# Gate and up products of the FFN with high and low activation halves as one 512-column operand

## The reference

```
def swiglu(u, wg, wu, wd):
    return (jax.nn.silu(u @ wg) * (u @ wu)) @ wd        # wg, wu: 1024 x 2816, wd: 2816 x 1024
h = h + 0.5 * swiglu(rmsnorm(h, gain), wg, wu, wd)      # first block; the second also norms the result
```

## Time and profile before

| what | value |
|---|---|
| runs | 2073.89 us median of 3 (2067.85 to 2074.85) |
| profiled execution: span, first to last instruction | 2067.1 us; the profile has no time of its own beside it |
| mean granted clock of TensorE | 0.981 of full |
| TensorE, VectorE, ScalarE busy | 95%, 61%, 45% of the span |
| A tiles | 221 DMAs of 1024 KB, 5.7 us from issue to landing |
| B tiles | 181 DMAs of 512 KB, 3.5 us |
| TensorE's waits for act_hl | 1.7 us in all, once |

### The profile page before, as it was taken

How to read it: one execution, slowest core, us unless ns; L and a number is a source line. 1 busy time by engine, 2 the same in 40 slices (tenths; PEclk the granted TensorE clock), 3 DMA queues, 4 the chain that set the end, 5 groups by cost and what they waited for, 6 DMA issues and landing times.

```text
span 2067.1 us, 33713 instructions
## 1 busy us (share of the span) xinstructions
PE 1972.9 (95%) x13218; PEld 1807.7 (87%) x13218; DVE 1256.9 (61%) x1668; ACT 936.1 (45%) x1283; POOL 107.3 (5%) x137
## 2 busy tenths in 40 slices
PE   8999999989998999999999888999999998989998
PEld 7998899989997778999899886799989998878998
DVE  5655655565445546555655698665566555766555
ACT  5444544354445535443544445444454445445443
POOL 0000000000000000000000046100000000010000
PEclk9999999999999999999999998999999999999999
DMA  6444454434452125545444332264445443424442
GB/s 260 186 183 183 147 195 182 173 143 183 183 194 93 50 82 196 199 183 193 171 185 183 140 142 86 82 245 188 187 151 197 183 185 121 143 100 180 191 188 94
DMA packets 60863, 338.35 MB, mean 164 GB/s; under 512 B 6800, under 2 KB 7056, under 8 KB 32384
## 3 DMA queue, kind: packets, MB, share of 16 engines
q1 hardware_dynamic: 59040, 330.00, 42.4%
q0 software_dynamic: 1760, 7.47, 1.1%
HBM read 336.39 MB, written 1.05 MB: 163 GB/s over the span
## 4 chain that ended last, share of the span: by engine, by line
PE 88%; DVE 6%; ACT 3%; DMA 1%; issue 1%; POOL 0%; SPq 0%; DVEq 0%; ACTq 0%
PE X L1312 56%; PE Y L1312 31%; DMA rawA<-in_wa 1%; DVE arena L1147 1%; DVE loA L881 1%; ACT hiA L485 1%; ACT xh L510 1%; PE X L1338 1%; DVE h L942 1%; DVE xl L910 1%; DVE xs L935 0%; POOL rstd L412 0%; ACT Y L495 0%; ACT arena L627 0%; PE Y L1632 0%
## 5 line engine op out<-in xcount | busy, mean ns | idle before, releaser
L1312 PE MATMUL X<-xh,hiA 128*128 128x256 f32 x2944 | 837.5, 284 | 13.0 <-DVE xl L910 11.9
L1312 PE MATMUL X<-xl,hiA 128*128 128x256 f32 x2944 | 836.5, 284 | 0.0
L1312 PE MATMUL X<-xh,loA 128*128 128x256 f32 x2944 | 836.4, 284 | 0.0
L881 DVE TENSOR_TENSOR loA<-rawA,hiA 128x2048 fp32r<-128x2048 f32 x221 | 509.2, 2304 | 309.5 <-ACT hiA L485 309.5
L1312 PEld LDWEIGHTS X<-xh,hiA 128*128 128x128 f32 x2944 | 568.1, 193 | 23.2 <-issue 9.9
L1312 PEld LDWEIGHTS X<-xl,hiA 128*128 128x128 f32 x2944 | 568.1, 193 | 6.2
L1312 PEld LDWEIGHTS X<-xh,loA 128*128 128x128 f32 x2944 | 568.0, 193 | 0.0
L485 ACT ACTIVATE hiA<-rawA 128x2048 fp32r<-128x2048 f32 (+1 forms) x233 | 424.9, 1824 | 81.1 <-PE Y L1312 51.6
L1312 PE MATMUL Y<-hiB,act_hh 128*128 128x512 f32 x704 | 276.8, 393 | 1.7 <-DVE act_hl L990 1.7
L1312 PE MATMUL Y<-loB,act_hh 128*128 128x512 f32 x704 | 275.9, 392 | 0.0
L1312 PE MATMUL Y<-hiB,act_hl 128*128 128x512 f32 x704 | 274.0, 389 | 0.0
(11 more groups left out here) (208 smaller groups left out, 1720.0 us busy)
## 6 DMA issues: line engine op xcount, KB each, us to landing
rawA<-in_wa SPq DMA_DIRECT2D x221, 1024.0 KB, 5.7
rawB<-in_wb SPq DMA_DIRECT2D x181, 512.0 KB, 3.5
row_gain<-in_rows POOLq DMA_DIRECT2D x8, 512.0 KB, 4.6
arena<-in_gla POOLq DMA_DIRECT2D x1, 1280.0 KB, 8.6
h<-in_x SPq DMA_DIRECT2D x2, 512.0 KB, 4.3
rawA<-in_wa SPq DMA_DIRECT2D x2, 512.0 KB, 6.7
out<-h SPq DMA_DIRECT2D x2, 512.0 KB, 2.6
arena<-in_pool POOLq DMA_DIRECT2D x1, 768.0 KB, 7.9
```

What stands on the lines that cost most here:

```text
L881: nc.vector.tensor_tensor(loA[p][:, :], rawA[p][:, :], hiA[p][:, :].bitcast(f32), ALU.subtract).then_inc(a_lo, 1)
L1312: return say(nc.tensor.matmul(*args, **kw))
```

## The change

`xh` and `xl` become the two halves of one buffer `xc`, so that a k-slice's high and low activations lie side by side as 512 columns. For each k-slice of gate and up, one matmul takes these 512 columns against the high weights into a whole PSUM bank, and a second one takes the 256 high columns against the low weights into the right half of the same bank. The sum of the bank's halves is the product. On eviction ScalarE copies the right halves of both banks (gate and up, 2 x 256) to SBUF, and VectorE adds the left halves to them; scaling by `root` is one operation over both (2 x 256). There is no semaphore for gate alone any more. The other stages keep `by_weights`; renamed semaphores and two call sites are left out of the diff.

```
-        xh = sb("xh", [P, KD, TOKENS], f32r)
-        xl = sb("xl", [P, KD, TOKENS], f32r)
+        xc = sb("xc", [P, KD, 2, TOKENS], f32r)
+        xh, xl = xc[:, :, 0, :], xc[:, :, 1, :]
...
+        act_g = arena[:, 12256:13280].rearrange("p (a b c) -> p a b c", b=2, c=TOKENS)
+        act_lo = arena[:, 13280:14304].rearrange("p (a b c) -> p a b c", b=2, c=TOKENS)
...
@@ scalar engine, step of an FFN
+                    act.wait_ge(up_psum, e + 1 + f)
+                    nc.scalar.activation(act_lo[:, p, :, :], X[:, 2 * p:2 * p + 2, TOKENS:512], ACT.Copy
+                                         ).then_inc(part_copied, 1)
                     if s["late"]:
-                        act.wait_ge(gate_scaled, NF * s["deferred"] + 1 + f)
-                        nc.scalar.activation(act_s[:, p, :], act_s[:, p, :], ACT.Silu).then_inc(silu_done, 1)
+                        act.wait_ge(pair_scaled, NF * s["deferred"] + 1 + f)
                     else:
-                        act.wait_ge(gate_psum, e + 1 + f)
-                        nc.scalar.activation(act_s[:, p, :], X[:, 2 * p, 0:TOKENS], ACT.Silu).then_inc(silu_done, 1)
+                        act.wait_ge(parts_added, e + 1 + f)
+                    nc.scalar.activation(act_s[:, p, :], act_g[:, p, 0, :], ACT.Silu).then_inc(silu_done, 1)
@@ vector engine, step of an FFN
                     split_B(b + f, (b + p) % 2)
-                    up = X[:, 2 * p + 1, 0:TOKENS]
+                    dve.wait_ge(part_copied, e + 1 + f)
+                    nc.vector.tensor_tensor(act_g[:, p, :, :], X[:, 2 * p:2 * p + 2, 0:TOKENS], act_lo[:, p, :, :],
+                                            ALU.add).then_inc(parts_added, 1)
                     if s["late"]:
                         if first:
                             dve.wait_ge(root_done, s["deferred"] + 1)
-                        dve.wait_ge(gate_psum, e + 1 + f)
-                        nc.vector.tensor_tensor(act_s[:, p, :], X[:, 2 * p, 0:TOKENS], root, ALU.mult
-                                                ).then_inc(gate_scaled, 1)
-                        dve.wait_ge(up_psum, e + 1 + f)
-                        nc.vector.tensor_tensor(act_h[:, p, :], up, root, ALU.mult).then_inc(up_scaled, 1)
-                        dve.wait_ge(up_scaled, NF * s["deferred"] + 1 + f)
-                        up = act_h[:, p, :]
+                        dve.wait_ge(parts_added, e + 1 + f)
+                        nc.vector.tensor_tensor(act_g[:, p, :, :], act_g[:, p, :, :],
+                                                root.unsqueeze(1).broadcast_to([P, 2, TOKENS]), ALU.mult
+                                                ).then_inc(pair_scaled, 1)
+                        dve.wait_ge(pair_scaled, NF * s["deferred"] + 1 + f)
                     dve.wait_ge(silu_done, e + 1 + f)
-                    dve.wait_ge(up_psum, e + 1 + f)
-                    nc.vector.tensor_tensor(act_h[:, p, :], act_s[:, p, :], up, ALU.mult
+                    nc.vector.tensor_tensor(act_h[:, p, :], act_s[:, p, :], act_g[:, p, 1, :], ALU.mult
                                             ).then_inc(prod_done, 1)
@@ tensor engine
+            def by_pair(bank, wh, wl, k, first, last):
+
+                mm(bank, wh, xc[:, k, :, :].rearrange("p a b -> p (a b)"), start=first, stop=False)
+                return mm(bank[:, TOKENS:512], wl, xh[:, k, :], start=False, stop=last)
...
-            def first_block(s, out_ap, other_ap, done, other_done):
+            def first_block(s, out_ap, other_ap, done, product=by_weights):
...
-                        ins = by_weights(dst, wh[:, j, k, :], wl[:, j, k, :], k, k == 0, k == KD - 1)
-                    if j or done:
-                        ins.then_inc(other_done if j else done, 1)
+                        ins = product(dst, wh[:, j, k, :], wl[:, j, k, :], k, k == 0, k == KD - 1)
+                ins.then_inc(done, 1)
...
-                        ins = by_weights(X[:, 2 * p + j, 0:TOKENS], wh[:, j, k, :], wl[:, j, k, :], k,
-                                         k == 0, k == KD - 1)
-                    ins.then_inc((gate_psum, up_psum)[j], 1)
+                        ins = by_pair(X[:, 2 * p + j, :], wh[:, j, k, :], wl[:, j, k, :], k,
+                                      k == 0, k == KD - 1)
+                    if j:
+                        ins.then_inc(up_psum, 1)
...
-                first_block(s, X[:, 0, 0:TOKENS], X[:, 1, 0:TOKENS], gate_psum, up_psum)
+                first_block(s, X[:, 0, :], X[:, 1, :], up_psum, by_pair)
```

More of the change, by code:

```diff
@@ L244, in build @@
         y_part, h_done = sem("y_part"), sem("h_done")
-        root_psum, root_done, gate_scaled, up_scaled = (sem(n) for n in ("root_psum", "root_done", "gate_scaled", "up_scaled"))
+        root_psum, root_done = sem("root_psum"), sem("root_done")
+        part_copied, parts_added, pair_scaled = sem("part_copied"), sem("parts_added"), sem("pair_scaled")
         vec_chain = sem("vec_chain")
-        gate_psum, up_psum, silu_done = sem("gate_psum"), sem("up_psum"), sem("silu_done")
+        up_psum, silu_done = sem("up_psum"), sem("silu_done")
         prod_done, prod_hi, prod_lo = sem("prod_done"), sem("prod_hi"), sem("prod_lo")
@@ L1666, in hyb @@
                 transposes(s, 1)
-                first_block(s, X[:, 0, 0:TOKENS], X[:, 0, TOKENS:512], None, sg_psum)
+                first_block(s, X[:, 0, 0:TOKENS], X[:, 0, TOKENS:512], sg_psum)
                 pe.wait_ge(phase_loaded["hyb"], 16)
@@ L1798, in gla @@
                 transposes(s, 1)
-                first_block(s, X[:, 0, 0:TOKENS], X[:, 0, TOKENS:512], None, gqk_psum)
+                first_block(s, X[:, 0, 0:TOKENS], X[:, 0, TOKENS:512], gqk_psum)
                 pe.wait_ge(phase_loaded["gla"], 48)
```

## The result

The changed kernel takes 2085.02 us (median of 7, 2083.01 to 2088.64), the one before 2073.89 (2067.44 to 2077.67): ratio 1.0073, 95% interval 1.0059 to 1.0087. It is 0.7% slower, where 2060.4 and faster was forecast.

The account below looks back on a forecast made before the run. TensorE's time per step was taken to bound the FFNs, with eviction counting at their ends. Six late FFNs -11.3, FFN 0 -1.0, FFN 2 -4.2 make -16.5 us; clock +3 gives 2060.4 us, range 2043 to 2084.

Parts of the forecast that it names:

- chain: Eviction after gate and up: from the start of ScalarE's copy to the start of the low part, 3.49 us.
- ring: Repeating eviction and splitting cycle of ScalarE and VectorE inside an FFN: 8.01 us, within TensorE's step of 8.24.
- first wait: First step of a late FFN: TensorE waits 1.7 us for eviction, its down product 1.19 later than before.
- last wait: Last step of an FFN: TensorE waits 2.1 us for the final low part, in FFN 2 1.5.
- the first term: TensorE's gate/up products in each FFN step: a k-slice takes 0.343 us instead of 0.359, saving 0.26 us a step.
- late FFN: FFN with deferred root, 7 of 8; six counted at -1.89 us each: steps -5.20, start +1.19, end +2.12.
- the 3 us allowed for: Clock term: two falls of TensorE's clock behind new waits, 1.7 us of work each, +3; bounds 0 and +24.
- the period: Sign in mid-FFN: TensorE's step repeats every 8.24 us; above 8.34 the prediction is wrong, the saving too small.
- A: Rival: products cost almost nothing beyond their columns, k-slice 0.355; +16 us, with clock +19, 2093 us, slower; chance 0.12.
- B: Rival: the ring is longer than TensorE's step; at 8.3 us it costs 22 us, 2082 us, slower; chance 0.12.
- C: Rival: most new waits are followed by a half-clock stretch, 20 or 24 us, 2077 to 2081 us; chance 0.10.
- D: Rival: k-slice 0.340 and down products at 0.227, saving 0.34 us a step; -30 us, 2044 us; chance 0.14.

Follow-up runs that it names:

- experiment 7: Changed kernel with the second product of each k-slice also taking all 512 columns, low x low added: 2367.67 us, one execution.
- experiment 2: New eviction alone, with three 256-column products per k-slice written into the bank's halves: 2094.94 us, ratio 1.0149 to the kernel before.
- experiment 3: Changed kernel with the 256-column product added into the bank's left half, not the right: 2088.56 us, ratio 1.0083 to the kernel before.

## Why the prediction was wrong

**What was right.** What bounds the kernel; that eviction is hidden in mid-FFN and not at its ends; and the sizes there: chain 3.49 (measured 3.57 and 3.51), ring 8.01 (8.02), first wait 1.7 (1.53 to 1.59), last wait 2.1 (2.05 and 2.06). Only FFN 0's first down product came 0.7 later than summed (31.53 instead of 30.79): its A tile landed 0.7 later (ScalarE begins to split it at 25.21, before at 24.55). The clock fell during that wait of 5.3 us, which is what FFN 0's body lost.

**The step that failed** is the first term: "I take 0.343, nearer to the hopeful end". A k-slice takes 0.3525, so a step saves 0.113 us and not 0.26. In a late FFN that is -2.2 instead of -5.2 in 20 steps, beside +3.5 at its ends (forecast 3.3): +1.3 instead of -1.9. Over eight FFNs, 162 steps that count, it is 24 us, and 2060.4 + 24 = 2084, next to the 2085.02 measured. That the two meet so closely is partly luck. The sum with 0.113 in it puts the profiled execution 10 us above before's, and it is 16.0 above: the clock cost more than the 3 us allowed for (6.4 at last steps alone), FFN 0's start 0.7, and FFN 5 gave 1.3 back. The medians are only 11.1 apart: I had put before's 6.8 us between span and median on the new kernel too, and there it is 1.9. This made up for the clock.

The value lay between the ends I had named, 0.340 and 0.355, near the bad one. Both reasons for the other choice were false. "The first 256 behind a 512 is exactly the neighbourhood" was true of one product (113), not of what follows. And the 0.23 to 0.24 of 512-column products does not come only behind 48 short ones: one short product is enough. The rows held a warning: the short products pay 6.7 ns each in a run (120 against 113), and the first long ones behind them 27 ns in all (2.747 us for twelve against 2.720 in experiment 7). But no row had an alternating stream. Measured, its mean surcharge is 353 - 340 = 13 ns for two products, 6.7 each again; so a removed product saved just one such surcharge, 360 - 353.

Of the signs named, the period did show it, 8.39 where 8.34 was the limit; the last waits stayed at 2.06, and the mean clock came to 0.975, just at its limit.

By the formula of the Trainium skill (TensorE: Matmul & The Clock Gate, "Back-to-back issue gap"), which the page calls the gap of an isolated matmul, a saved product was estimated at 2.5 ns. Measured are 6.7, so it is too small here, but its direction, that merging is worth little and the sum comes out slower, was the better guide.

**The rivals.** A is nearest to what happened: its mechanism with a slice of 0.355, its size too large (2093). Its turning point, a saving of 0.16 us a step, fits: 0.113 is below it, and the kernel is slower. B didn't occur, with 0.37 us to spare instead of 0.23. C occurred in part: the profiled execution has 22 stretches at the lower level where before had 16; four of the 22 are at last waits and one at FFN 0's first, where two were allowed for. D did not occur; by its own figures two of its terms are -3.5 and -6.0 and not -3.6 and -5.8, which leaves its sum at -30. The range ended at 2084.0, since I let it leave A out.

## What to carry to other kernels

Price a merge of matmuls by the mean start distance of the mixed stream it makes, from the rows on both sides of each change of size, and take the bad neighbour as likely as the good one. Where a cheaper inner step lengthens the chain behind it, count the places where nothing covers that chain (here 15) times its growth, and keep the old form in just these steps. Then try the order: products of one size in long runs were worth as much again as the merge itself (2058 to 2042 us).

## What the hardware showed

Here each product loads 128 columns of weights. A stream of 512-column products only is 226.7 ns apart, of 256-column ones 120, and the first 256 behind a run of 512 is 113, half of 226.7; in the alternating stream, where each 256 follows a 512, they are 118, 120 and 113. A 512-column product behind 256-column ones pays, up to the fifth (233, 236, 228, 232, 231), and it did so in each place tried: into the next bank of X, into Y, with the short product in the left or the right half. The merged but alternating stream never gets out of it. The runs show this dependence on order; what in TensorE causes it they do not, and as every product has its own weight load in all of them, the load's part in it can't be told.

The clock: waits of one length were followed by a fall or not. Of the seven last waits of 2.05 or 2.06 us it was four in the changed kernel, one in experiment 2 and five in experiment 3; of the six first waits of 1.46 to 1.59, none in any of the three.
